# FFN up-projections with 7 block products for 8, token-major, in a hybrid conformer/SSD encoder on one Trainium2 core

## The reference

```python
D_MODEL = 1024; SEQ = 256; DEPTH = 2; D_FF = 2816

def _rms_norm(x, g):
    y = xf * lax.rsqrt(jnp.mean(xf * xf, axis=-1, keepdims=True) + EPS)
    return (y * g).astype(x.dtype)

def _swiglu(x, w_up, w_down):
    a, b = jnp.split(x @ w_up, 2, axis=-1)
    return (jax.nn.silu(a) * b) @ w_down

for i in range(DEPTH):
    x = x + 0.5 * _swiglu(_rms_norm(x, ffn1_norm[i]), ffn1_w_up[i], ffn1_w_down[i])
    ...                       # the mixer
    x = x + 0.5 * _swiglu(_rms_norm(x, ffn2_norm[i]), ffn2_w_up[i], ffn2_w_down[i])
```

## Time and profile before

| | |
|---|---|
| time, median of 3 runs | 2877.98 us (2876.42 to 2883.38) |
| the profiled execution | span of 2875.2 us from its first to its last instruction |
| PE (matmul) busy | 2849.9 us, 99% |
| DVE busy | 1864.9 us, 65% |
| ACT busy | 1324.5 us, 46% |
| POOL busy | 140.4 us, 5% |
| mean DMA traffic | 105 GB/s |

### The profile page before, as it was taken

The page is one execution under the profiler, slowest core; times in us unless marked ns, Lnnn a source line. Parts: engine busy times, 40 slices in busy tenths (PEclk is TensorE's granted clock), DMA queues, the critical chain, the costliest instruction groups (busy, mean ns, idle before and its releaser), DMA issues.

```text
span 2875.2 us, 34509 instructions
## 1 busy us (share of the span) xinstructions
PE 2849.9 (99%) x12886; PEld 2309.2 (80%) x12886; DVE 1864.9 (65%) x2387; ACT 1324.5 (46%) x1833; POOL 140.4 (5%) x237
## 2 busy tenths in 40 slices
PE   7999999999999999999999999999999999999998
PEld 6888887777778888888888888877777788888886
DVE  5444489999996554443543435899999866554445
ACT  5322356767754434222342223676766634442223
POOL 1000002110001000000000000100110010000000
PEclk9999999999999999999999999999999999999999
DMA  6333234333336333333333333333333463333332
GB/s 199 101 94 103 77 94 109 105 103 97 104 111 187 89 102 95 95 95 97 94 109 96 95 95 95 98 94 98 103 110 93 116 180 95 96 106 96 98 92 84
DMA packets 532025, 301.88 MB, mean 105 GB/s; under 512 B 17039, under 2 KB 521751, under 8 KB 531895
## 3 DMA queue, kind: packets, MB, share of 16 engines
q1 hardware_dynamic: 511888, 261.65, 32.1%
q0 software_dynamic: 17296, 37.29, 4.3%
q10 hardware_dynamic: 2711, 1.21, 0.2%
HBM read 280.54 MB, written 19.53 MB: 104 GB/s over the span
## 4 chain that ended last, share of the span: by engine, by line
PE 99%; ACTq 0%; ACT 0%; DMA 0%; DVE 0%; issue 0%
PE bank L1302 93%; PE bank L1475 2%; PE bank L1519 1%; PE bank L1527 0%; PE bank L1453 0%; PE bank L1441 0%; PE bank L1554 0%; PE bank L1459 0%; DMA dtbA<-in_ssd_A_log 0%; PE bank L1343 0%; PE bank L1421 0%; ACTq L537 0%; PE bank L1359 0%; PE bank L1465 0%; ACT o_tm L896 0%
## 5 line engine op out<-in xcount | busy, mean ns | idle before, releaser
L907 DVE TENSOR_TENSOR wlo<-wraw,whi 128x1024 fp32r<-128x1024 f32 x496 | 605.5, 1223 | 262.5 <-ACT whi L519 252.7
L1302 PE MATMUL bank<-uhi,whi 128*128 128x512 f32 x1952 | 770.0, 394 | 4.1 <-DVE ulo L963 3.3
L1302 PE MATMUL bank<-hhi,whi 128*128 128x512 f32 x1952 | 769.7, 394 | 0.0
L1302 PE MATMUL bank<-ulo,whi 128*128 128x512 f32 x1952 | 760.6, 390 | 0.0
L1302 PE MATMUL bank<-uhi,wlo 128*128 128x512 f32 x1952 | 760.3, 390 | 0.0
L1302 PE MATMUL bank<-hlo,whi 128*128 128x512 f32 x1952 | 759.9, 389 | 0.0
L1302 PE MATMUL bank<-hhi,wlo 128*128 128x512 f32 x1952 | 759.8, 389 | 0.0
L519 ACT ACTIVATE whi<-wraw 128x1024 fp32r<-128x1024 f32 x496 | 521.6, 1054 | 423.3 <-PE bank L1302 410.4
L1302 PEld LDWEIGHTS bank<-uhi,whi 128*128 128x128 f32 x1952 | 366.8, 188 | 94.8 <-issue 13.4
L1302 PEld LDWEIGHTS bank<-hhi,whi 128*128 128x128 f32 x1952 | 366.4, 188 | 89.9 <-issue 13.4
L1302 PEld LDWEIGHTS bank<-ulo,whi 128*128 128x128 f32 x1952 | 366.9, 188 | 77.2 <-issue 2.9
(11 more groups left out here) (212 smaller groups left out, 1900.7 us busy)
## 6 DMA issues: line engine op xcount, KB each, us to landing
wraw<-in_ffn_w_up SPq DMA_DIRECT2D x179, 512.0 KB, 3.8
wraw<-in_w_in SPq DMA_DIRECT2D x160, 512.0 KB, 4.0
wraw<-in_ffn_w_down SPq DMA_DIRECT2D x64, 512.0 KB, 3.7
wraw<-in_ssd_w_out SPq DMA_DIRECT2D x32, 512.0 KB, 4.3
wraw<-in_ffn_w_down SPq DMA_DIRECT2D x32, 384.0 KB, 3.3
y_spill<-yz POOLq DMA_DIRECT2D x16, 512.0 KB, 3.2
yraw<-y_spill POOLq DMA_DIRECT2D x32, 256.0 KB, 3.5
wraw<-in_conf_w_out SPq DMA_DIRECT2D x16, 512.0 KB, 4.7
```

Of the source, the lines that this page charges most:

```text
L907: v_.tensor_tensor(wlo[:, t % RING, :], wraw[:, t % RING, :], f32(whi[:, t % RING, :]), ALU.subtract).then_inc(lo_ready, 1)
L1302: ins = t_.matmul(out, a[:, slot, w], b[:, at + k, :], start=start and k == 0 and a is whi and b is hi, stop=stop and k == nk - 1 and a is ...
```

## The change

The 2816 features of a and of b are cut into five groups of 512 and a tail of 256 (`FG`, `TAIL_W`). In a group the up-projection is a product of blocks, 2 by 2 by 2: tokens of the first and second request, even and odd tiles of the inner dimension, features of a and of b. It is done with seven block products for eight. Their operands are sums of the blocks: the sums of activations are made once per FFN by DVE (`s_sums`, L1186 to L1196) and split by ACT and DVE into `shi` and a low part (`s_high`, `s_low`). The sums of weight blocks are made in place by DVE, in `low_part` (L1119), eight per group, each 128 by 1024. The raw blocks lie in a buffer `blk` of four quarters, which SP's `load_quarter` fetches in halves of 512 KB; `wraw` keeps the tail's and the down-projections' slabs.

The up-projection is now token-major: the stationary operand is a 128 by 128 piece of the activations and the moving one 512 features of a weight (`token_major`, L1711). A block product is 24 matmuls on two slabs, in two halves t of 128 tokens, 12 matmuls each. The first slab of a product is released after 18 matmuls, the second after 24. Three partial results per token half are carried in `CA`, `CB`, `CC` (ACT copies them out of PSUM, DVE adds, `c_ready`). The silu takes the norm as ACT's per-partition scale, and one DVE instruction multiplies the rest (L1298). Since h is then token-major, PE turns every 128 features of it by four transposes (`turn`, L1746) into a PSUM bank, from which ACT makes the high part (`h_high`, L729) and DVE the low part (`h_low`, L1214). Group g-1 is turned during group g: two tiles after its product 0, two after its product 1. Banks 6 and 7 serve for both pairs. The last group's four are turned inside the last down-projection.

The down-projection is cut differently: 2 tiles (the tail) after group 0, 4 tiles after each of the groups 1 to 3, 8 tiles at the end. It stays feature-major and has as many matmuls as before, and adds to `xf` at L1343 through banks 6 and 7. The FFNs' `stats` is four matmuls with one column of ones instead of one with 512 columns. Loops of the FFN are unrolled.

The diff, cut to its core (of ACT's, DVE's and PE's part the order of a group):

```diff
-    PARTS = [(0, 8), (8, 8), (16, FT - 16)]
-    FFN_SLABS = 2 * FT + KD * len(PARTS)
+    GW = 512
+    FG = 5
+    PRODUCTS = 7
+    TAIL_W = 2 * P
+    TAIL_AT = FG * GW
+    assert FF == TAIL_AT + TAIL_W and KD == 8
+    UP_AT = [4, 20, 38, 56, 74]
+    D_TAIL = 18
+    D_AT = [34, 52, 70]
+    D_LAST = 88
+    FFN_SLABS = 96
...
+            def load_quarter(L, f, g, q, h):
+
+                group = (L * 2 + f) * FG + g
+                odd, b = divmod((B11, B12, B21, B22).index(q), 2)
+                if group:
+                    before = up_base(group - 1)
+                    if q == B11:
+                        sp.wait_ge(t_sum, 8 * (group - 1) + 7 + h)
+                    else:
+                        sp.wait_ge(lo_ready, before + {B21: 8, B12: 10, B22: 12}[q] + h + 1 + RING)
+                k = L * KD + odd + 4 * h
+                col = b * FF + g * GW
...
+            def high_part(t):
+
+                if t >= DEPTH * NSLAB:
+                    return
+                if t in block_slab:
+                    group, j = block_slab[t]
+                    summed = {2: 1, 3: 5, 4: 3, 6: 7}.get(j // 2)
+                    if summed is None:
+                        act.wait_ge(*quarter_in(group, PRODUCT_OF[j // 2], j % 2))
+                    else:
+                        act.wait_ge(t_sum, 8 * group + summed + j % 2)
+                else:
+                    act.wait_ge(raw_in[t % RING], 16 * plain_count[t])
...
+                    def event(n, t):
+                        if t == 0:
+                            act.wait_ge(half_done, half_of(FI, g, n))
+                        else:
+                            act.wait_ge(slab_done, b + 2 * n + 2 + RING)
+                        if n == 0:
+                            act.wait_ge(h_ready, FI * H_PIECES + (4 if g == 0 else 4 * g + 3 + t))
+                            a_.activation(CA[:, t, :], bank[X[t]][:, :], ACT.Copy).then_inc(snap, 1)
+                        if n == 1 and (g or t < 2):
+                            h_high(L, f, 2 + 4 * (g - 1) + t if g else t, h[0], t, T_BANKS[t])
+                        if n == 2:
+                            a_.activation(CC[:, t, :], bank[Y[t]][:, :], ACT.Copy).then_inc(snap, 1)
+                            if g:
...
+                    for n in range(PRODUCTS):
+                        high_part(b + 2 * n + 3)
+                        event(n, 0)
+                        high_part(b + 2 * n + 4)
+                        event(n, 1)
+
+                up(0)
+                for j in range(2):
...
+            def low_part(t):
+
+                if t >= DEPTH * NSLAB:
+                    return
+                dve.wait_ge(hi_ready, t + 1)
+                v_.tensor_tensor(wlo[:, t % RING, :], raw_of(t), f32(whi[:, t % RING, :]), ALU.subtract).then_inc(lo_ready, 1)
+                if t in block_slab:
+                    group, j = block_slab[t]
+                    h = j % 2
+                    if j < 8:
+                        q, other = ((B11, B12), (B12, B22), (B11, B22), (B11, B21))[j // 2]
+                        if j < 4:
+                            dve.wait_ge(*quarter_in(group, other, h))
+                        if j in (2, 3):
...
+            def h_low(L, f, tile, h, which, j, b):
+
+                n = (L * 2 + f) * H_TILES + tile + 1
+                hi = h[which][:, j, :]
+                dve.wait_ge(hhi_ready, n)
+                v_.tensor_tensor(h[which][:, 4 + j, :], bank[b][:, :], f32(hi), ALU.subtract).then_inc(hlo_ready, 1)
...
-                for part, (p0, n) in enumerate(PARTS):
-                    with dve.Fori(0, n // 2) as i:
-                        for j in range(2):
-                            PI = L * (2 * FT) + (f * FT + p0 + j) + i * 2
-                            split(s4 + i, 2 * j)
-                            dve.wait_ge(slab_done, (s4 + i) * 4 + 2 * j + 1 + RING)
-                            v_.tensor_tensor(fa[:, j, :], bank[2 * j][:, :], rbc[:, :], ALU.mult).then_inc(fa_ready, 1)
-                            split(s4 + i, 2 * j + 1)
...
+                    def event(n, t):
+
+                        if n == 1:
+                            done(n, t)
+                            dve.wait_ge(snap, group * 6 + 1 + t)
+                            v_.tensor_tensor(CA[:, t, :], bank[Z[t]][:, :], CA[:, t, :], ALU.add).then_inc(c_ready, 1)
+                            if g or t < 2:
+                                h_low(L, f, 2 + 4 * (g - 1) + t if g else t, h, 0, t, T_BANKS[t])
+                        if n == 2 and g:
+                            h_low(L, f, 4 * g + t, h, 0, 2 + t, T_BANKS[2 + t])
+                        if n == 4:
+                            done(n, t)
+                            dve.wait_ge(snap, group * 6 + 3 + t)
+                            v_.tensor_tensor(CC[:, t, :], bank[X[t]][:, :], CC[:, t, :], ALU.add).then_inc(c_ready, 1)
...
+                            if t == 1:
+                                piece(0, 0)
+                        if n == 6:
+                            piece(t, 1 - t)
...
+                        event(n, 0)
+                        low_part(b + 2 * n + 4)
+                        event(n, 1)
+
...
+                def down(d, half, part, slabs, each):
+
+                    for j in range(slabs):
+                        low_part(S + d + j + AHEAD)
+                        if j == 0:
+                            last_piece(L, f, UP_AT.index(d - 2 * PRODUCTS))
+                        for i in range(each):
+                            m = j * each + i
+                            if i < each - 1:
+                                dve.wait_ge(half_done, FI * HALVES + half + j * (each - 1) + i + 1)
+                            else:
+                                dve.wait_ge(slab_done, S + d + j + 1 + RING)
+                            dve.wait_ge(x_done, xb + part * KD - KD + m + 1)
+                            v_.scalar_tensor_tensor(out=xf[:, m, :], in0=bank[6 + m % 2][:, :], scalar=0.5,
                                                     in1=xf[:, m, :], op0=ALU.mult, op1=ALU.add).then_inc(x_done, 1)
-                    s4 = s4 + KD // 4
...
+                def token_major(out, act_hi, act_lo, w_at, start, stop):
+
+                    for a, w in ((act_hi, whi), (act_hi, wlo), (act_lo, whi)):
+                        ins = t_.matmul(out, a, w[w_at], start=start and a is act_hi and w is whi,
+                                        stop=stop and a is act_lo, skip_group_check=True)
+                    return ins
...
+                def turn(g, j, b):
+
+                    tile = 2 + 4 * g + j if g is not None else j
+                    if g is None:
+                        pe.wait_ge(h_ready, FI * H_PIECES + 4)
+                    else:
+                        pe.wait_ge(h_ready, FI * H_PIECES + 4 * g + 8)
+                        if b >= 6:
+                            pe.wait_ge(x_done, xb + KD * (min(g, FG - 2) + 1))
+                        if j >= 2 and g < FG - 1:
+                            pe.wait_ge(hlo_ready, FI * H_TILES + tile - 1)
+                    for c in range(NC):
+                        src = h5[:, c, chunk(j)] if g is None else h_piece(g, c, j)
+                        ins = t_.transpose(bank[b][:, chunk(c)], src, ident[:, :])
+                    ins.then_inc(t_ps, 1)
+
...
+                    def product(n, out, start):
+
+                        for t in range(2):
+                            bank_free(n, t)
+                            for i in range(4):
+                                slab = b + 2 * n + i // 2
+                                if t == 0 and i % 2 == 0:
+                                    pe.wait_ge(lo_ready, slab + 1 + RING)
+                                if t == 0 and n == 2 and g == 0:
+                                    pe.wait_ge(s_ready, FI * 8 + 2 * i + 2)
+                                w_at = (slice(None), slab % RING, slice((i % 2) * GW, (i % 2 + 1) * GW))
+                                ins = token_major(bank[out[t]][:, :], *operand(n, i, t), w_at, start and i == 0, i == 3)
+                                if t == 1 and i == 1:
+                                    ins.then_inc(slab_done, 1)
+                            ins.then_inc(slab_done if t else half_done, 1)
+
+                    product(0, X, True)
+                    for j in range(2):
+                        turn(g - 1 if g else None, j, T_BANKS[j])
+                    product(1, Z, True)
+                    if g:
+                        for j in range(2, 4):
+                            turn(g - 1, j, T_BANKS[j])
+                    product(2, Y, True)
+                    product(3, X, False)
...
+                def down(d, part, nk, each):
+
+                    pe.wait_ge(hlo_ready, FI * H_TILES + (2 + 4 * part - 4 + nk if part else nk))
+                    for m in range(KD):
+                        j, mm = divmod(m, each)
+                        if mm == 0:
```

(5 more changed lines are left out.)

568 lines of the change are left out of this document (402 added, 166 removed).

## The result

The changed kernel takes **2909.5 us** (median of 4 runs, 2903.2 to 2918.6), against 2877.5 us (2876.4 to 2883.4) for the kernel before, timed beside it: a ratio of 1.0109, with a 95% interval of 1.0085 to 1.0133. It is slower by 1.1%. The forecast was 2890 us and slower by 0.4%; the measured time lies inside the range, but 32 us from the kernel before where 12 were forecast. The profiled execution is one of the four, with 2905.7 us and a span of 2904.0, 28.8 us above the span before. The prediction's sum was +11.8.

What follows compares the result with a forecast made beforehand. PE was taken as the bound. In us: -108.9 matmuls, +38.7 transposes, +1 stats, +52 fourth tile, +22 tail, +1 last tiles, +6 start make +11.8, so 2887; with 2.8 for the median, forecast 2890, range 2850 to 2922.

Steps and rivals of the forecast that it cites:

- The saving of matmuls: Up-projection groups on PE: 480 matmuls fewer at 0.2268 us each, 108.9 us saved, all on the path.
- the transposes: Turning h on PE: 88 tiles, four transposes each, 0.44 us per tile, 38.7 us added; bounds 31 to 53 us.
- the waits of the fourth tile: Groups 1 to 4: PE waits for DVE to read tile 2 from bank 7, 3.25 us 16 times, 52 us.
- the tail: Down-projection after group 0: PE waits for DVE's additions, 3.9 and 1.6 us per FFN, 22 us in all.
- The start: Program start: PE waits 4.9 us behind DVE's activation sums, 1.2 more at the first turned tile, 6 us together.
- The first turned tile's 1.2 us: Part of the start's 6 us: PE waits 1.2 us more there for DVE's backlog.
- The last tiles: Last four tiles, turned in the last down-projection: first low part 0.3 us late for PE, 1 us in all.
- The clock stays at 1.00 between the start and the end: Expected sign in the changed kernel's profile; a drop of the clock's row in mid-program would show the prediction wrong.
- waits for SP's loads: Sign of being wrong: PE waiting for anything from SP's loads; DMA was costed at nothing.
- DVE keeps up: Rival: DVE clears its backlog before PE asks, fourth-tile waits fall to 1.3 us, tail waits go; 2837 us, chance 0.15.
- The new matmuls are dearer: Rival: 3744 matmuls with activations as stationary operand cost 5 ns more each, 19 us; 2909 us, chance 0.06.
- The clock falls: Rival: PE's clock drops in the 20 new gaps, 1.4 us each, 28 us in all; 2918 us, chance 0.17.

Runs made afterwards that it cites:

- e1_early_split: Changed kernel with ACT's copy and DVE's low part of the first two turned tiles moved ahead of the waits for product 1: 2846.1 us, ratio 0.9892.
- e5_no_sums: Changed kernel with the 160 sums of weight blocks each replaced by a sum of 8 words, waits and order kept: 2879.6 us, timed once.
- e4_fill: Changed kernel with 272 matmuls of unread result put in the gaps before fourth turned tiles and in the tails, waits kept: 2892.6 us, ratio 1.0057.
- e6_start: Changed kernel with DVE making slab 3's low part before the first three sets of activation sums at the start: 2910.2 us, single execution.
- e2_tail_banks: Changed kernel with four PSUM banks instead of two for the tail's down-projection after group 0: 2892.6 us, ratio 1.0051.
- e3_both: Changed kernel with both the early split of the turned tiles and four banks in the tail's down-projection: 2823.1 us, ratio 0.9813.

## Why the prediction was right, and where not

- **Direction and mechanism: right.** The saving of matmuls (0.227 us each, in both roles), the transposes, the waits of the fourth tile (3.09 us by its row and 3.25 with the end of the matmul before, for a predicted 3.25, 16 times) and of the tail (20.7 us and 22.0, for a predicted 22) came as counted. One operation's place, shown by e1_early_split, decides the sign of the whole change; e5_no_sums shows that the wait is DVE's queue.
- **The start:** 5.8 us for one low part, predicted 4.9: the 15 activation sums take from 32.76 to 39.05 us on DVE, 6.3 us where 5.4 were counted. The first turned tile's 1.2 us is not in the list of waits. The sum, 6, was right.
- **The last tiles:** 0.4 us for 1.
- **The step that failed: "The clock stays at 1.00 between the start and the end."** The sum gave the clock nothing, and put up to 28 us of it into a rival with a chance of 0.17. In the profiled execution it fell eight times and cost 15 to 17 us, and e4_fill, with the gaps filled, is 17 us faster by the medians. A fall is some 2 us, where 1.4 was counted; there were 8 of them, where the rival had priced 20. The forecast missed the median by 19.5 us, and the lost clock is most of that. The fault was in the choice: the sum should have carried the term, say for the tails, since their gaps were predicted at 3.9 us, longer than the 3.2 us of the earlier trace rows, behind which the clock was already low. The rival was no alternative to the forecast but an addition to it.
- **A row misread.** The prediction says that the transposes ahead of the first wide matmuls had not raised the clock. The kernel before shows that they had:

```profile
9.16 5.35 PE L1329 MATMUL bank<-ident,x_tm 128*128 128x128 f32 x24 [9.16 <-DMA x_tm<-in_x_sample]
...
16.69 1.09 PE L1329 MATMUL bank<-ident,x_tm 128*128 128x128 f32 x8
```

  The first 24 start every 0.21 us, the last eight every 0.11, with nothing but transposes between, and the earlier trace rows has the clock at 1.00 in the wait behind them and at 0.52 after it. The mean of 386 ns mixes the two. The price of 1.4 us doesn't rest on this.
- **An omission:** the wait at L1910, 2.8 us once. The prediction named waits for SP's loads as a sign of being wrong; this load is POOL's, and it did not look at it.
- **What is left over.** Waits +77.6, work -69.2 and clock +15 to +17 make +23 to +25 of the measured +28.8. The matmuls' ends ahead of 25 more waits, 0.16 us each, are an estimated 4 more, so at most 2 us are left that I can't place.
- **The rivals.** *DVE keeps up* falls: 16 of 16 waits are there. *The new matmuls are dearer* falls: 27.25 us for 120. *The clock falls* holds in part: 8 falls instead of the 20 priced (7 of them at those 20 gaps, one at the start).

## What to carry to other kernels

With orders written by hand, ask of every result that another engine will overwrite or wait for: which waits and which operations stand ahead of it in the program of the engine that drains it? Here a 0.7 us operation stood behind a wait for work that came later, and cost 49 us; moving it cost nothing. Before pricing a wait on PE, add what the clock may take behind it, and look at stretches of a few microseconds for it, since a page in slices of 72 us doesn't show it.

## What the runs showed of the hardware that was not expected

Whether the granted clock falls after a gap is not fixed by the length of the wait. Waits of 3.7 us with no matmul in them: 4 falls of 4 in the changed kernel, in e1_early_split and in e6_start. Waits of 3.09 us between transposes: 3 of 16 in the changed kernel and in e6_start, and 9 of 16 in e2_tail_banks. Waits of 2.03 us between transposes in e5_no_sums: 7 of 16. Waits of 2.0 to 3.3 us for `LB` in all kernels: 6 of 8. Waits of 1.1 to 1.7 us in the tails of these five kernels: none of 20. The four timed executions of the changed kernel are spread over 15 us, from 2903 to 2919, where e2_tail_banks, e3_both and e4_fill stay within 2 to 6; the slowest has the lowest mean clock (0.986 against 0.990 to 0.992). With the transposes on either side (0.44 us each) the pause around a 2.03 us wait is about 2.9 us without a wide matmul, and 7 of 16 of these are followed by a fall, while 33 of the 48 pauses of about 4 us around the 3.09 us waits are not. What decides a given gap stays open, and so does what makes `LB` late in some executions; neither was tried. More banks for the turned tiles, and the sums of weight blocks on POOL (5% busy), weren't tried either.
